# Four orders exchanged in a two-layer encoder kernel: VectorE's rotations, mask and row maxima against its convolution taps, ScalarE's first exponentials against a copy, TensorE's projection against the convolution mean

## What is computed

```python
h = x @ w_in + b_in                                  # 1024 -> 1792 columns
c = causal_depthwise_conv(a * sigmoid(g), conv_w, conv_b)      # 256 channels, 31 taps
c = silu(layer_norm(c, conv_ln_g, conv_ln_b))
q, k = partial_rotary(q, pos), partial_rotary(k, pos)          # 8 query, 2 key/value heads of 64
att = sliding_window_sink_attention(q, k, v, sinks)            # chunks of 64, window 128
gm = spatial_gating(gelu(h[..., OFF_GMLP:]), ...)
x = layer_norm(alpha * x + concatenate([c, att, gm]) @ w_out + b_out)
x = layer_norm(alpha * x + moe_ffn(x, ...))                    # 16 experts, top 2
```

## Time and profile before

| | us |
|---|---|
| median of 3 runs | 1115.88 |
| lowest, highest | 1112.0, 1120.95 |
| the profiled execution's own time | 1118.77 |
| its span (first to last instruction) | 1117.0 |

### The profile page before, as it was taken

The page is one execution under the profiler, slowest core; times in us unless marked ns, Lnnn a source line. Parts: engine busy times, 40 slices in busy tenths (PEclk is TensorE's granted clock), DMA queues, the critical chain, the costliest instruction groups (busy, mean ns, idle before and its releaser), DMA issues. The chain is left out here.

```text
span 1117.0 us, 15296 instructions
## 1 busy us (share of the span) xinstructions
PE 977.4 (88%) x4780; PEld 801.3 (72%) x4780; DVE 809.9 (73%) x956; ACT 648.0 (58%) x720; POOL 527.0 (47%) x295
## 2 busy tenths in 40 slices
PE   5998999599999999999279989995999999999950
PEld 4866778478888888888168767784788888888840
DVE  2996766687877777787568957565878787777737
ACT  4324722377878878787213247222788787888820
POOL 3535354056564646565215453540555656464621
PEclk9998998599999999999679989985899999999985
DMA  8521193299999999953803211832999999999535
GB/s 277 191 82 40 46 336 137 70 332 355 369 376 363 381 361 377 365 215 110 244 27 114 75 48 38 324 135 77 333 374 376 363 363 371 360 369 369 230 124 138
DMA packets 122511, 268.99 MB, mean 241 GB/s; under 512 B 10608, under 2 KB 26128, under 8 KB 121968
## 3 DMA queue, kind: packets, MB, share of 16 engines
q1 hardware_dynamic: 110192, 244.00, 60.3%
q0 software_dynamic: 12288, 24.60, 6.9%
HBM read 263.39 MB, written 24.64 MB: 258 GB/s over the span
## 5 line engine op out<-in xcount | busy, mean ns | idle before, releaser
L1557 POOL TENSOR_TENSOR wl<-w_down,wh 128x2048 fp32r<-128x2048 f32 x33 | 151.6, 4594 | 169.9 <-ACT wh L978 169.9
L1066 DVE TENSOR_TENSOR wl<-w_gate,wh 128x2048 fp32r<-128x2048 f32 x71 | 166.1, 2340 | 54.1 <-ACT wh L978 28.0
L1066 DVE TENSOR_TENSOR wl<-w_up,wh 128x2048 fp32r<-128x2048 f32 x66 | 151.1, 2292 | 29.8 <-ACT wh L978 29.3
L734 PE MATMUL bank<-wh,xTh 128*128 128x512 f32 x528 | 144.8, 397 | 0.2 <-ACT wh L978 0.2
L978 ACT ACTIVATE wh<-w_down 128x2048 fp32r<-128x2048 f32 x66 | 126.8, 1920 | 31.4 <-PE bank L734 31.4
L734 PE MATMUL bank<-wl,xTh 128*128 128x512 f32 x528 | 143.4, 394 | 1.6 <-DVE wl L1066 1.6
L734 PE MATMUL bank<-wh,xTl 128*128 128x512 f32 x528 | 143.4, 394 | 1.0 <-DVE xTl L1066 1.0
L978 ACT ACTIVATE wh<-w_up 128x2048 fp32r<-128x2048 f32 x66 | 126.6, 1918 | 29.7 <-PE bank L752 24.8
L1498 POOL TENSOR_TENSOR wl<-w_gate,wh 128x2048 fp32r<-128x2048 f32 x17 | 78.1, 4599 | 133.3 <-ACT wh L835 132.9
L978 ACT ACTIVATE wh<-w_gate 128x2048 fp32r<-128x2048 f32 x66 | 126.5, 1916 | 7.6 <-PE bank L752 7.6
L1066 DVE TENSOR_TENSOR xTl<-bank,xTh 128x512 fp32r<-128x512 f32 (+1 forms) x168 | 89.7, 573 | 47.7 <-issue 22.7
(11 more groups left out here) (222 smaller groups left out, 1764.4 us busy)
## 6 DMA issues: line engine op xcount, KB each, us to landing
w_up<-in_exp_w_up SPq DMA_DIRECT2D x32, 2048.0 KB, 12.4
w_down<-in_exp_w_down SPq DMA_DIRECT2D x32, 2048.0 KB, 10.4
w_gate<-in_exp_w_gate SPq DMA_DIRECT2D x32, 2048.0 KB, 12.3
w_gate<-in_w_in SPq DMA_DIRECT2D x14, 1024.0 KB, 5.5
w_gate<-in_w_out SPq DMA_DIRECT2D x8, 1024.0 KB, 5.0
x_rows<-xtok POOLq DMA_DIRECT2D x8, 512.0 KB, 3.0
w_gate<-in_rows_mix SPq DMA_DIRECT2D x2, 1536.0 KB, 6.3
w_up<-in_x_t SPq DMA_DIRECT2D x4, 512.0 KB, 7.3
```

The source lines that it names most:

```text
L734: mm = pe.matmul(bank[piece][:, :], xgT[m][:, 4 * (i % 2) + k, :], w[q][:, k, :], start=(i % 2 == 0 and n == 0 and k == 0), stop=(i % 2 == ...
L1066: return dve.tensor_tensor(out, src, high.bitcast(F32), ALU.subtract)
L1557: pool.tensor_tensor(wl[s][:, :], slot[r][p][:, cols], wh[s][:, :].bitcast(F32), ALU.subtract)\
```

## The change

Four moves and nothing else; no instruction is added or taken away.

- DVE: `rope(l, 3)` is followed by `rope(l, 4)`, the mask and the memset of `wsT`, and only then by taps 20 to 25. The copy of the values and `softmax_max(l, 0)` come before taps 26 to 30, and `join_taps(l, 1)` after them.
- ACT: `softmax(l, 0)` comes before `odd_copy(l, 1)`.
- PE: `channels(5, 1)` comes before `conv_mean(l)`.

```diff
                 turn_values(l)
                 scores(l, 0)
+                channels(5, 1)
                 conv_mean(l)
-                channels(5, 1)
                 scores(l, 1)
...
                 gated(l, 10, gvT[:, 0, :])
+                softmax(l, 0)
                 odd_copy(l, 1)
-                softmax(l, 0)
                 conv_squares(l)
...
-                for n, hi in enumerate((8, 14, 20, 26)):
+                for n, hi in enumerate((8, 14, 20)):
                     rope(l, n, qr[:, n, :])
                     taps(1, hi - (4 if n == 0 else 6), hi)
+                rope(l, 3, qr[:, 3, :])
                 rope(l, 4, kr)
                 for g in range(2):
                     link(dve.memset(bank[4 + g][0:64, :].rearrange("p (h k) -> p h k", h=4)[:, :, 0:64], -1e30))
                 dve.sem_inc(mask_set, 1)
                 dve.memset(wsT[64:P, :, 0:64], 0.0).then_inc(ws_zeroed, 1)
-                taps(1, 26, TAPS)
+                taps(1, 20, 26)
 
                 dve.wait_ge(v_turned, l + 1)
                 link(dve.tensor_copy(vmem[:, 0, :, :], bank[6][:, :].rearrange("p (j c) -> p j c", j=TT)))
                 dve.sem_inc(v_set, 1)
+                softmax_max(l, 0)
+                taps(1, 26, TAPS)
                 join_taps(l, 1)
-                softmax_max(l, 0)
```

## The result

| | before | after |
|---|---|---|
| median, 20 runs each | 1113.13 | 1124.55 |
| lowest, highest | 1110.24, 1120.95 | 1117.27, 1127.71 |
| the profiled execution's own time | 1118.77 | 1122.95 |
| its span | 1117.0 | 1121.1 |

The ratio is 1.0073 with a 95% interval of [1.0053, 1.0094]: the kernel became 6 to 10 us slower, within 1%, but clearly. A second set of ten runs of the changed kernel, beside runs of before on the same chip, gave 1.0060 [1.0032, 1.0087]. The forecast was 2 us slower in the likeliest case, with 1109 to 1122 us as its outer range; the median of 1124.55 lies above that range.

A forecast was written before the change was run, and what follows sets the result against it. PE was taken as the busiest engine, mostly named by the waits. `conv_var` +1.0 us a layer, up to +2.1, taken as +2.2 for two layers on the 1115.88 us median, gave 1118.0 us; range 1109 to 1122.

The forecast's parts named there:

- the term of 1.9 us for the row maxima: On DVE, block 0's maxima, now ahead of the last five taps, were to delay the joined taps by 1.9 us.
- The fifth rotation is held, the mask gains nothing: DVE's L1073 of rotation 4 waits for POOL's low part, lasting 4.8 us to 82.0; first scores stay at 83.9.
- The join: PE sees the joined taps, and starts the mean, at 95.9 instead of 89.11: 4.05 taps, 1.9 maxima, 0.7 ACT's copy.
- The exponentials ahead of ScalarE's copy cost nothing: On ACT, exponentials run from 91.1 to 94.1, over before the last tap, so the copy is not delayed.
- The projection: On PE, projection (5, 1) starts behind the scores at 86.9 and ends at 93.1 (early bound) to 94.7 (late bound).
- The clock at the mean: PE idles about 2.8 us ahead of the mean, which then runs at half clock, taking 3.8 us; chance 0.50.
- From the mean to `conv_var`: Mean from 95.9, DVE's centring and normalizing, block 1's scores and maxima, then `conv_var` at 105.9.
- `conv_var`: +1.0 to +2.1 a layer was forecast: `conv_var` at 105.9 instead of 104.89, up to +2.1 with transposes at half clock; over 3 us would refute the forecast.
- That a shift of `conv_var` is passed on in full: Behind `conv_var`, PE's projections, scores and output product follow in order and weight loads move along, so any shift stays.
- From the profile to the median: Shift read from the profiled execution (1118.77 us), +2.2 us for two layers, was added to the median of 1115.88 us.
- DVE ahead of POOL: Rival: L1073 of rotation 4 isn't held, `conv_var` 3.0 us a layer earlier, 1109.8 us; chance 0.12.
- half clock beyond `conv_var`: Rival: PE's projections (6, 0) and (6, 1) at half clock, 1127.5 us with the first alone, 1137 with both; chance 0.03.

The follow-up runs named there:

- e9: Changed kernel, with GpSimd's value copies and residual scaling waiting until the row maxima of block 0 are done; 1116.86 us, ratio 1.0024 to the kernel before.
- e4: Changed kernel, with one wait added so that GpSimd's low part of weight piece 7 starts after the mask; 1109.91 us, ratio 0.9967 to the kernel before.
- e11: Changed kernel with GpSimd's low part of weight piece 7 held until the mask is set, repeated for an undisturbed profile; 1111.48 us, ratio 0.9981 to the kernel before.
- e6: Changed kernel without any edit, run again for a second profile; 1120.94 us, ratio 1.0060 to the kernel before.
- e10: Kernel before plus early rotation and mask, early projection, GpSimd's piece 7 wait, and maxima, join, value copy in that order after the taps; 1111.99 us, ratio 0.9974.
- e3: Kernel before with only values and maxima ahead of the last taps and exponentials ahead of ScalarE's copy; 1125.30 us, ratio 1.0088.
- e5: Kernel before without any edit, run again for a second profile; 1115.66 us over 10 runs.

## Why the prediction was right or wrong, point by point

The sign and the class (slower, within 1%) came out as forecast. The size did not: +2.2 us was forecast and about 8 came, and the outer range of 1109 to 1122 us was missed. The step that failed is the term of 1.9 us for the row maxima in the sum for the join: in their new place they took 4.67 us in layer 0 and 3.04 in layer 1, held beside GpSimd's transfers and scaling. e9, which takes that hold away, is 0.24% or 2.7 us slower than before, near the sum's 2.2; its interval (-0.9 to 6.1 us) is wide.

- **The fifth rotation is held, the mask gains nothing: right.** 4.76 and 4.77 us in the two layers where 4.8 was expected, first scores at 3.39 as before. e4 and e11 show that this, and not the order as such, is what the first move lost: without the hold the mean comes 4.1 us earlier.
- **The join: the step that failed, by the size of one term.** The mean was to start 6.8 us later than before (4.05 taps, 1.9 maxima, 0.7 ScalarE's copy). It starts 9.5 us later in layer 0 and 7.8 in layer 1 (18.11 and 16.46 against 8.63). The taps and the copy were right. The 1.9 us of the maxima were not: I took them from an occurrence where nothing held them (102.02) and wrote of POOL's transfers and scaling only that no engine waits for them. But they are released by the copy of the values, which the change puts directly ahead of the maxima, and beside them the small instructions took 2.8 and 1.1 us more. Before, the same instructions were held too (`s_max` at 93.0, 4 us after the maxima began at 89.0), but there they ran beside the mean, ahead of nothing that the convolution needs; the change put them ahead of the join. The trace of before had their price in rows that I did not use (90.42 and 91.31 above). e9 takes the hold away and the mean moves by 2.77 and 1.15.
- **The exponentials ahead of ScalarE's copy cost nothing: right.** In layer 0 they ran 95.25 to 98.3 and the copy started at 98.79, behind the last tap.
- **The projection: right.** It ran without a gap behind the scores and ended at 96.4, or at 94.8 once the 1.56 us by which this execution started later are taken off, 0.1 us past my late bound of 94.7. The clock was back at full at 93.
- **The clock at the mean: right in layer 0, wrong in layer 1.** Half clock after idle 3.77 us, full clock after 2.11. From the earlier trace rows, where 2.09 us had been followed by half clock, I had expected both to fall. In the second profile (e6) both did: half clock after 5.35 and 3.72 us.
- **From the mean to `conv_var`: 10.0 us was forecast, 9.2 and 7.7 came in the first profile, 9.5 and 9.9 in the second.** I had priced the scores of block 1 at half clock (4.15 us); in layer 0 they took 2.56 us, at full clock.
- **`conv_var`: +1.0 to +2.1 a layer was forecast; +2.9 and -0.1 in the first pair of profiles, +4.4 and +3.2 in the second.** The second pair is beyond the 3 us that I had named as a sign that the forecast is wrong. That the first pair adds up to 2.8 us, near the forecast of 2.1, is luck: the mean came 2.7 and 1.0 us later than forecast, and the way from it to `conv_var` was 0.8 and 2.3 us shorter. The holds of the maxima are the part that was missing; without them (e9) `conv_var` is 2.2 and 0.8 us earlier than in the first profile of the changed kernel.
- **That a shift of `conv_var` is passed on in full: right for the change, not in general.** The way to the router's first product was 78.8 us in both layers before and 78.7 and 78.8 after; in e10 it grew to 81.96.
- **From the profile to the median: a second size that was off.** The profiled execution of before was at the upper end of its runs (1118.77, median 1113.13), that of after below its median (1122.95, 1124.55). Subtracting two such profiles gives 4.2 us, of which 1.6 us is the start of the execution; the medians give 11, the ratio 8. My own sum added 2.2 us to a median of three runs (1115.88) that was itself 2.7 too high. The median overstates the difference: the 20 times of before have a gap between 1116.7 and 1119.0 with 15 below it, so their median sits in the lower group, while 14 of the 20 times after are above 1121; the means differ by 8.7 us. The +5.2 us of four profiles lie inside the interval of e6 (3.6 to 9.7 us) and just below that of the first comparison (5.9 to 10.5), the +7.5 of the second pair inside both. What makes up the rest between 5.2 and 8 is open; two profiles a kernel are too few to say.
- **The rivals.** DVE ahead of POOL was given 1109.8 us, 3.0 us a layer or 0.5% faster than before. e4 and e11, which make it true, are 0.3 and 0.2% faster: the mean came at 14.05 and 12.39 where the rival had 11.3, since the maxima are held there as well. The other side (half clock beyond `conv_var`) did not occur: the mixing stage behind it took 77.2 to 78.8 us in all four profiles.

## What to carry to other kernels

Before VectorE's work is reordered, lay GpSimd's timeline beside the new one, not the old one: here an instruction with one operand in PSUM ran freely under a GpSimd instruction, the one put in its place did not, and one added wait on GpSimd turned 0.6 to 0.7% slower into 0.2 to 0.3% faster. Cost an instruction from an occurrence that has the same neighbours on the other engines as its new place. Try each part of a change by itself: here one part gained 0.4% and two cost 0.9%, and when the path in front gets shorter, look at what is queued ahead of the next small instruction on the slow engine (in e10 the way behind `conv_var` grew by 3.2 us of the 6.8 gained, and moving the scaling gave 2.7 of them back in layer 0).

## What the runs showed of the hardware

- An 8-column L1118 of VectorE, 0.17 us when nothing holds it, took 1.46, 1.31, 0.86, 0.72 or 0.25 us. It had started between 0.36 us before and 0.85 us after the start of GpSimd's scaling, the TENSOR_SCALAR behind the transfers, and each time it ended 1.10 us after that start (93.40 against 92.30, 656.31 against 655.21 in the kernel after; 91.28 against 90.18, 651.31 against 650.21 before; 89.68 against 88.58 in e3). An L1120, which has one tensor input, was then held in layer 0 until 2.85 us after that start (to 95.15; one of the four scalings takes 2.83 us), but not in layer 1 of either kernel, where it started at the same distance (1.14 us behind the start, 1.13 in layer 0); in layer 1 of e3 it was held again, 0.68 us, to 2.86 us after. The Trainium skill, page "SBUF — State Buffer", section "Who interferes with whom", says that a TENSOR_SCALAR of VectorE can enter a mode with two ports and then contends with GpSimd, and the hold in layer 0 agrees; why it was free in layer 1 of the two kernels no run here shows.
- Idle time of TensorE ahead of the mean, and the time of its four matmuls: 0, 0.98, 1.02, 1.38 and 2.11 us of idle time, 1.88 to 1.98 us (full clock); 3.11 and 3.12 (e5), 3.72, 3.77, 4.03, 4.12, 5.35 and 6.53 us and more, 3.27 to 3.78 us (half clock for most or all of it). The border is not a length of idle time alone: 2.09 us ahead of 124.62 were followed by half clock, and ahead of the mean of before (2.23 and 1.87 us) the clock had been low since the first scores.
